# Low parts of 48 weight units: GpSimd's subtraction or an accumulating DMA, in a float32 conformer trunk

## The reference, cut to what matters

```
mod = silu(c) @ ada_w + ada_b                       # 6 vectors of 2048: shifts, scales, gates
h = rms_norm(x, norm1_g) * (1 + sc1) + sh1
u = h @ w_in + b_in ; a, gt = split(u)              # 2048 x 4096
u = a * sigmoid(gt)
u = causal depthwise conv, 31 taps + b_dw
u = silu(layer_norm(u)) ; y = u @ w_out + b_out     # 2048 x 2048
x = x + g1 * y
h = rms_norm(x, norm2_g) * (1 + sc2) + sh2
x = x + g2 * (square(relu(h @ w1)) @ w2)            # 2048 x 8192, 8192 x 2048
out = rms_norm(x, final_g)
```

## Time and profile before

| what | value |
|---|---|
| median of three runs | 2128.62 us |
| the profiled execution's own time | 2129.86 us |
| its span (first to last instruction) | 2128.1 us |
| mean granted TensorE clock | 0.968 |
| TensorE matmul busy | 2004.2 us (94%) x8640 |
| VectorE busy | 1097.9 us (52%) |
| ScalarE busy | 667.8 us (31%) |
| GpSimd busy | 451.1 us (21%) |
| DMA | 299.58 MB, mean 141 GB/s |

### The profile page before, as it was taken

The page is one execution under the profiler, slowest core; times in us unless marked ns, Lnnn a source line. Parts: engine busy times, 40 slices in busy tenths (PEclk is TensorE's granted clock), DMA queues, the critical chain, the costliest instruction groups (busy, mean ns, idle before and its releaser), DMA issues.

```text
span 2128.1 us, 22314 instructions
## 1 busy us (share of the span) xinstructions
PE 2004.2 (94%) x8640; PEld 1632.2 (77%) x8640; DVE 1097.9 (52%) x1133; ACT 667.8 (31%) x717; POOL 451.1 (21%) x197
## 2 busy tenths in 40 slices
PE   5889999888987889999999999999999999999996
PEld 2668888656766767888888888888888888888885
DVE  5959989978698984323323332332332332232243
ACT  4334545453232222232132123123213213312332
POOL 3647999923433230000000000000000000000001
PEclk8999999979998999999999999999999999999998
DMA  9962433315866572222222222222222222222212
GB/s 399 394 258 101 158 138 118 119 60 197 341 262 246 202 292 91 87 99 99 99 99 99 99 87 91 100 96 99 99 99 99 99 99 80 101 95 99 99 59 79
DMA packets 45933, 299.58 MB, mean 141 GB/s; under 512 B 4688, under 2 KB 4688, under 8 KB 10960
## 3 DMA queue, kind: packets, MB, share of 16 engines
q1 hardware_dynamic: 45904, 299.24, 37.5%
HBM read 295.03 MB, written 4.19 MB: 141 GB/s over the span
## 4 chain that ended last, share of the span: by engine, by line
PE 72%; DVE 13%; POOL 6%; issue 4%; DMA 3%; ACT 2%; SPq 0%; DVEq 0%; POOLq 0%; ACTq 0%
PE ps L313 23%; PE ps L314 23%; PE ps L315 23%; DVE adar L760 3%; POOL wlo L1055 3%; DMA adar<-ada 3%; DVE adar L772 2%; DVE raw L772 1%; POOL pacc L1094 1%; DVE hlo L766 1%; PE ps L386 1%; DVE ps L843 1%; POOL adar L1098 1%; DVE wlo L783 1%; ACT whi L472 1%
## 5 line engine op out<-in xcount | busy, mean ns | idle before, releaser
L313 PE MATMUL ps<-hhi,whi 128*128 128x512 f32 (+1 forms) x1792 | 708.6, 395 | 61.7 <-DVE hlo L766 29.8
L314 PE MATMUL ps<-hlo,whi 128*128 128x512 f32 (+1 forms) x1792 | 704.9, 393 | 0.0
L315 PE MATMUL ps<-hhi,wlo 128*128 128x512 f32 (+1 forms) x1792 | 704.4, 393 | 0.0
L472 ACT ACTIVATE whi<-raw 128x2048 fp32r<-128x2048 f32 x176 | 336.1, 1910 | 680.5 <-PE ps L315 680.5
L313 PEld LDWEIGHTS ps<-hhi,whi 128*128 128x128 f32 x1792 | 341.4, 191 | 141.0 <-issue 56.2
L313 PE MATMUL ps<-dhi,whi 128*128 128x512 f32 x1024 | 399.8, 390 | 11.7 <-DVE dlo L1020 11.7
L314 PE MATMUL ps<-dlo,whi 128*128 128x512 f32 x1024 | 399.6, 390 | 0.0
L315 PE MATMUL ps<-dhi,wlo 128*128 128x512 f32 x1024 | 399.3, 390 | 0.0
L315 PEld LDWEIGHTS ps<-hhi,wlo 128*128 128x128 f32 x1792 | 340.9, 190 | 72.2
L314 PEld LDWEIGHTS ps<-hlo,whi 128*128 128x128 f32 x1792 | 341.6, 191 | 70.7
L783 DVE TENSOR_TENSOR wlo<-raw,whi 128x2048 fp32r<-128x2048 f32 x127 | 291.0, 2292 | 95.6 <-ACT whi L472 95.6
(11 more groups left out here) (142 smaller groups left out, 951.3 us busy)
## 6 DMA issues: line engine op xcount, KB each, us to landing
raw<-w SPq DMA_DIRECT2D x176, 1024.0 KB, 4.8
adar<-ada SPq DMA_DIRECT2D x80, 1024.0 KB, 5.0
raw<-ada SPq DMA_DIRECT2D x16, 1024.0 KB, 8.5
xb<-xT SPq DMA_DIRECT2D x8, 1024.0 KB, 9.6
out<-xb SPq DMA_DIRECT2D x5, 512.0 KB, 4.3
out<-xb SPq DMA_DIRECT2D x6, 256.0 KB, 3.8
csb<-c SPq DMA_DIRECT2D x1, 1024.0 KB, 4.9
pr<-par SPq DMA_DIRECT2D x1, 368.0 KB, 14.3
```

The lines of the kernel that those rows point to most:

```text
L313: pe.matmul(out, whi[:, slot, t], xhi, start=first, stop=False, skip_group_check=True)
L314: pe.matmul(out, whi[:, slot, t], xlo, start=False, stop=False, skip_group_check=True)
L315: return pe.matmul(out, wlo[:, slot, t], xhi, start=False, stop=last, skip_group_check=True)
L472: act.activation(whi[:, q % WS, :], raw_slot(q), ACT.Copy).then_inc(whi_done, 1)
```

## The change

Units 10 to 57 (48 of the 49 that GpSimd subtracted) get their low part in another way: ScalarE writes the negated high part into `wlo` after it has written `whi`, and an accumulating DMA that GpSimd issues adds `raw` to it. Its semaphores are `lo_in[0..1]`. TensorE starts a unit at `whi_done` and waits for the low part only before the products that use it, which now stand last in every unit: in `outer_unit` all high-weight products with the high activations of a chunk, then those with its low part, for both chunks, and then the 16 low-weight products; in `inner_unit` 32 and then 16. The order of the products is changed in all 176 units, the way of the low part in 48. The waits of SyncE's loads follow the same semaphores. Loops are cut so that no loop holds units of both kinds, and one GpSimd loop is written out.

```diff
-LO_POOL = W2_0 + 2
+DMA_LO = range(A1 + 2, W2_0 + 2)
...
+        def wait_lo(eng, q, off=0):
+            if q in DMA_LO:
+                eng.wait_ge(lo_in[q % WS], 16 * ((q - DMA_LO.start) // WS + 1) + (16 // WS) * off)
+            else:
+                eng.wait_ge(wlo_done, (q + 1 if q < DMA_LO.start else q + 1 - len(DMA_LO)) + off)
...
             def load_unit(q, off=0):
-                sp.wait_ge(wlo_done, q - RAW + 1 + off)
+                wait_lo(sp, q - RAW, off)
...
+            def outer_unit(q, s, h0, j=0, i=None):
+                i, first = (0, s == 0 and j == 0) if i is None else (i, False)
+                pe.wait_ge(whi_done, 2 * i + (q + 2 * j + s + 1))
                 for kk in range(2):
-                    k = 4 * i + (2 * s + kk)
+                    k = 4 * i + (4 * j + 2 * s + kk)
+                    pe.wait_ge(hhi_done, k + (h0 + 1))
+                    for o in range(8):
+                        high(o, s, 8 * kk + o, ch(hhi, k), first and kk == 0)
                     pe.wait_ge(hlo_done, k + (h0 + 1))
                     for o in range(8):
-                        last = product(o, s, 8 * kk + o, ch(hhi, k), ch(hlo, k), first and kk == 0, False)
+                        high(o, s, 8 * kk + o, ch(hlo, k), False)
+                wait_lo(pe, q + 2 * j + s, 2 * i)
+                for kk in range(2):
+                    k = 4 * i + (4 * j + 2 * s + kk)
+                    for o in range(8):
+                        last = low(o, s, 8 * kk + o, ch(hhi, k), False)
                 last.then_inc(unit_done, 1)
...
+            def inner_unit(slot, bank, q, off=0):
+                pe.wait_ge(whi_done, off + (q + 1))
                 for k in range(KC):
-                    last = product(bank, slot, k, ch(hhi, k), ch(hlo, k), k == 0, k == KC - 1)
+                    high(bank, slot, k, ch(hhi, k), k == 0)
+                    high(bank, slot, k, ch(hlo, k), False)
+                wait_lo(pe, q, off)
+                for k in range(KC):
+                    last = low(bank, slot, k, ch(hhi, k), k == KC - 1)
                 last.then_inc(unit_done, 1)
...
                 act.activation(whi[:, q % WS, :], raw_slot(q), ACT.Copy).then_inc(whi_done, 1)
+                if q in DMA_LO:
+                    act.wait_ge(whi_done, q + 1 + off)
+                    act.activation(wlo[:, q % WS, :], f(whi[:, q % WS, :]), ACT.Copy, scale=-1.0
+                                   ).then_inc(neg_done, 1)
...
             def split_lo(q, off=0):
-                pool.wait_ge(whi_done, q + 1 + off)
-                pool.tensor_tensor(wlo[:, q % WS, :], raw[:, q % RAW, :], f(whi[:, q % WS, :]), ALU.subtract
-                                   ).then_inc(wlo_done, 1)
+                if q not in DMA_LO:
+                    pool.wait_ge(whi_done, q + 1)
+                    pool.tensor_tensor(wlo[:, q % WS, :], raw[:, q % RAW, :], f(whi[:, q % WS, :]), ALU.subtract
+                                       ).then_inc(wlo_done, 1)
+                    return
+                pool.wait_ge(neg_done, q - DMA_LO.start + 1 + off)
+                pool.dma_start(f(wlo[:, q % WS, :]), raw[:, q % RAW, :], accum_op=ALU.add
+                               ).then_inc(lo_in[q % WS], 16)
```

More of the change, by code:

```diff
@@ L134, in trunk_kernel @@
         wlo_done = sem("wlo_done")
+        neg_done = sem("neg_done")
+        lo_in = [sem(f"lo_in{i}") for i in range(WS)]
         unit_done = sem("unit_done")
@@ L266, in _ @@
             sp.wait_ge(ada_used, ADA0)
-            with loop(ET.SP, 0, 6) as i:
+            for s in range(2):
+                load_unit(A1 + 2 + 2 * s)
+                load_unit(A1 + 3 + 2 * s)
+                load_ada(2 * KC + s)
+            with loop(ET.SP, 0, 5) as i:
                 for s in range(2):
-                    load_unit(A1 + 2 + 2 * s, 4 * i)
-                    load_unit(A1 + 3 + 2 * s, 4 * i)
-                    load_ada(2 * KC + s, 2 * i)
+                    load_unit(A1 + 6 + 2 * s, 4 * i)
+                    load_unit(A1 + 7 + 2 * s, 4 * i)
+                    load_ada(2 * KC + 2 + s, 2 * i)
             a += ADA_A1
@@ L290, in _ @@
             assert a == ADA
-            load_unit(W2_0 + 2)
-            load_unit(W2_0 + 3)
-            with loop(ET.SP, 1, (NUNITS - W2_0) // RAW) as i:
+            for q in range(2, 6):
+                load_unit(W2_0 + q)
+            with loop(ET.SP, 0, (NUNITS - W2_0) // RAW - 2) as i:
                 for q in range(RAW):
-                    load_unit(W2_0 + q, 4 * i)
+                    load_unit(W2_0 + 6 + q, 4 * i)
+            load_unit(NUNITS - 2)
+            load_unit(NUNITS - 1)
             stores = [(fin_dve, n, min(2, FIN_POOL - n)) for n in range(0, FIN_POOL, 2)]
@@ L373, in _ @@
             outer_units(A0, 0)
-            with loop(ET.PE, 0, 6) as i:
+            for s in range(2):
+                pe.wait_ge(glu_done, 3 + s)
+                inner_unit(0, 2 * s, A1 + 2 * s)
+                inner_unit(1, 2 * s + 1, A1 + 2 * s + 1)
+            with loop(ET.PE, 0, 5) as i:
                 for s in range(2):
-                    pe.wait_ge(glu_done, 2 * i + (3 + s))
-                    inner_unit(0, 2 * s, 4 * i + (A1 + 2 * s + 1))
-                    inner_unit(1, 2 * s + 1, 4 * i + (A1 + 2 * s + 2))
+                    pe.wait_ge(glu_done, 2 * i + (5 + s))
+                    inner_unit(0, 2 * s, A1 + 4 + 2 * s, 4 * i)
+                    inner_unit(1, 2 * s + 1, A1 + 5 + 2 * s, 4 * i)
             for n, c in enumerate((KC - 2, KC - 1)):
@@ L426, in w2_unit, with w2_pairs @@
                             pe.wait_ge(dlo_done, wait_hidden + (k + 1))
-                        last = product(4 + 2 * (m % 2) + nn, m % 2, 8 * nn + k, ch(dhi, k), ch(dlo, k),
-                                       k == 0, k == BLK - 1)
+                        high(bank, m % 2, 8 * nn + k, ch(dhi, k), k == 0)
+                        high(bank, m % 2, 8 * nn + k, ch(dlo, k), False)
+                    if nn == 0:
+                        wait_lo(pe, q, off)
+                    for k in range(BLK):
+                        last = low(bank, m % 2, 8 * nn + k, ch(dhi, k), k == BLK - 1)
                 last.then_inc(unit_done, 1)
-            def w2_rest(b):
-                w2_unit(1, 16 * b + (W2_0 + 2))
+            def w2_pairs(b, q):
                 with loop(ET.PE, 1, 4) as i:
@@ L437, in w2_rest, with hidden_units @@
                         pe.wait_ge(x2_done, 16 * b + 4 * i + (2 * s - 1))
-                        w2_unit(s, 16 * b + 2 * i + (W2_0 + s + 1))
-            pe.wait_ge(wlo_done, W2_0 + 1)
+                        w2_unit(s, q + 2 + s, 16 * b + 2 * i - 2)
+            def hidden_units(b):
+                with loop(ET.PE, 0, 4) as i:
+                    for s in range(2):
+                        pe.wait_ge(relu_done, 8 * b + 2 * i + (BLK + s - 1))
+                        inner_unit(s, s, W2_0 + BLK + s, 16 * b + 2 * i)
+                pe.wait_ge(x2_done, 16 * b + 17)
+                w2_unit(0, W2_0 + 2 * BLK, 16 * b, 8 * b + BLK)
+            pe.wait_ge(whi_done, W2_0 + 1)
             pe.wait_ge(relu_done, 2)
@@ L445, in _ @@
                 for nn in range(2):
-                    last = product(4 + nn, 0, 8 * nn + k, ch(dhi, k), ch(dlo, k), n == 0, n == BLK - 1)
+                    high(4 + nn, 0, 8 * nn + k, ch(dhi, k), n == 0)
+                    high(4 + nn, 0, 8 * nn + k, ch(dlo, k), False)
+                    if n == 0 and nn == 0:
+                        wait_lo(pe, W2_0)
+                    last = low(4 + nn, 0, 8 * nn + k, ch(dhi, k), n == BLK - 1)
             last.then_inc(unit_done, 1)
             pe.wait_ge(relu_done, BLK)
[L449 to L457, removed]
+            w2_unit(1, W2_0 + 1)
+            w2_pairs(0, W2_0)
+            hidden_units(0)
+            with loop(ET.PE, 1, NBLK - 1) as b:
+                w2_unit(1, W2_0 + 2 * BLK + 1, 16 * b - 16)
+                w2_pairs(b, W2_0)
+                hidden_units(b)
+            w2_unit(1, W2_0 + 2 * BLK + 1, 16 * (NBLK - 2))
+            w2_pairs(NBLK - 1, W2_0)
             pe.wait_ge(ss2_done, KC)
@@ L1021, in _ @@
                                       ).then_inc(dlo_done, 1)
[L1022 removed]
+            dve.wait_ge(wlo_done, A1 + 2)
             with loop(ET.DVE, 0, NBLK - 1) as b:
@@ L1111, in _ @@
             a1_chunk(0, 1)
-            with loop(ET.Pool, 1, 4) as i:
+            for i in range(1, 4):
                 a1_chunk(i, 0)
@@ L1129, in _ @@
             c_sums(13)
-            for q in range(B0 + 2, LO_POOL):
+            for q in range(B0 + 2, DMA_LO.stop):
                 split_lo(q)
```

34 lines of the change are left out of this document (15 added, 19 removed).

## The result

The changed kernel takes 2158.6 us (median of 4, 2155.36 to 2160.9) against 2128.65 us (4 runs): ratio 1.0142, 95% interval 1.0126 to 1.0157, slower by 30 us. The forecast was 2143 us. The sign held, and most of the mechanism; one step failed: the stretch from B0's start to `x1` took 11.4 us more than before, where the sum had nothing. The profiled execution took 2155.36 us, the fastest of its four, 25.5 us above the profiled one of before.

What follows compares the result with a forecast made beforehand. Prediction: products bound A1 and the end; between 470 and 800 us `ada` loads and stalled VectorE reductions set the pace. Terms -1.9 + 0.4 + 18 - 1.4, less 2, gave +13 on 2129.86: 2143 us, range 2100 to 2190.

Steps and rivals of the forecast that it cites:

- The price: Each 1 MiB accumulating transfer was taken to occupy all DMA engines for 5.3 us, with 2.6 and 7.9 as ends.
- A0 and A1: Units 0 to 7 gain 1.9 us by product order; units 10 to 31 lose 0.4 us by a later convolution start.
- VectorE's stalls: GpSimd's subtraction stalls VectorE's two-input instructions; without it `ada` reductions stay at 2.28 us instead of up to 6.69.
- B0, up to unit 42: `x1` begins 5 us late, but lost stalls and a start without subtraction bring unit 42 forward: -1.5 us.
- Unit 36: In B0, TensorE starts at 518.0 instead of 522.85 us, but its low part comes at 529; about 3 us kept.
- B1: Seven more transfers make the last `ada` row 12 us later; a lost stall returns 4.2; C0's start +8 us.
- C0: Eight transfers beside the loads lengthen the stretch from 687 to 793 us to 116 instead of 106 us: +10.
- After W2: From the MLP's second matrix on, one stall goes and units 56 and 57 have early low parts: -1.4 us.
- -2 for shorter `hlo` waits: At the starts of B0 and C0, high products begin 0.7 us sooner and the slow clock ends sooner: -2 us.
- The cheap transfer: Rival: from B0 to C0 a transfer costs only 2.63 us and VectorE is free, giving 2102 us; chance 0.35.
- the low part comes late everywhere: Rival: TensorE waits before low products in all 48 units, about +60 us, 2190 us; chance 0.12 for dear or late.
- break-even price of 4.4 us: Transfer price at which the change neither gains nor loses, 2124 to 2136 us; chance 0.10 for a price near it.

Runs made afterwards that it cites:

- the plain copy: Changed kernel with a plain copy of `raw` into `wlo` instead of the accumulating transfer (output differs): 2114.48 us, 0.9935 of the kernel before.
- these transfers alone: New product order, with negation and accumulating transfer for units 42 to 57 only and GpSimd subtracting elsewhere: 2148.70 us, 1.0098 of the kernel before.
- without any maker: Changed kernel with its negations but neither transfer nor subtraction for the 48 low parts (output differs): 2084.39 us, 0.9788 of the kernel before.

## Why the prediction was right in kind and 15 us short

*The price.* Taken at 5.3 us, measured 5.20, and DMA's share from 530 to 790 us is 0.95, near full as the prediction required: right, and its three readings (2.6, 5.3, 7.9) were the right question, since the plain copy sits at 2.64. The Trainium skill's rule ("Collectives: The Full Stack", "The bandwidth ceiling: the fold count and why AG ≠ RS ≠ AR") that a reduce runs at half a copy's rate agrees with these two (1.97 times); its 31 GB/s, by which I had estimated 4.2 us, does not.

*A0 and A1* (-1.9 and +0.4). Unit 11's forward copy begins at 174.09 instead of 175.84 us: -1.75 of A0's -1.9. The convolution that began 11.24 us behind its `whi` begins 11.64 behind (338.67 against 327.03 us): +0.40 as worked out. B0 starts 0.8 us sooner, against -1.5, which is within what a mark can tell. For A1's end the number was luck: the prediction said that GpSimd's subtraction is one "that nobody waits for", and there the chain of before goes through it twice; the negation took its place.

*VectorE's stalls.* Reductions of 2282 to 2295 ns in all 51 from B0 to C0, with DMA at a share of up to 1.0 beside them: GpSimd was their whole cause. One reading beside it was wrong, without weight in the sum: of the 29.8 us in which TensorE waits for `hlo`, which the prediction named for 470 to 800 us, only 4.5 lie there.

*B0, up to unit 42* (-1.5). **This is the step that failed.** The prediction said that DMA near full would need "55 instead of 46 us, from 524 instead of 528", that `x1` begins 5 us late and unit 42 1.5 us early, and so let B1 start "from about 592 us as before". Measured: the chain starts at 518 and needs 67 us to `x1`; `x1` is 10.6 us late, unit 42 7.8 (609.2 us). First, the count was wrong, and the trace of before could have told it. I took 34 us for "ten rows and three units", by their number. But the window of the kernel before over that stretch says
```profile
528.00:574.00 46.00, 45.07 (x198) 36.91 (x198) 30.79 (x23) 8.08 (x5) 21.51 (x4) 1.00 0.82 315
```
0.82 x 46 = 37.7 us, the reloads of `xb` among them. And five transfers, not four, fall in the changed kernel's stretch from 518 on, as the one issued at 513.4 us is still under way: 37.7 + 5 x 5.2 = 63.7 us, where its window has 0.97 x 65 = 63. Second, even its own 5 us were not passed on: a lost stall and a start without a subtraction were set against them, for unit 42. But B1's rows follow from `x1`, which the `ada` rows alone set by then, and unit 42 could not use its early start, since TensorE waited 5.0 us for unit 41's low part (at 603.5 us).

*Unit 36.* Its low part was to keep TensorE waiting some 4 us; it waited 5.8.

*B1* (+12 - 4.2 = +8, from a start as before, 18 us behind `x1`) and *C0* (+10). From `x1` to C0 took 8.8 us more (9.8 with these transfers alone), from C0 to W2 8.7 more (8.3): both terms are right within 1.8 us. With `x1`'s 10.6 us at their head the two terms give C0 18.6 us late and W2 28.6; measured are 19.4 and 28.1. That a late B0 is not absorbed is the point of a full DMA: with GpSimd subtracting in B1 more than half of it was.

*After W2* (-1.4). From W2 to the end the profiled execution gained 2.6 us. Of the -2 for shorter `hlo` waits, 0.7 us shows at B0's start, where TensorE's wait fell from 5.65 to 4.93 us. It lies 25.5 us above the profiled execution of before, the medians 30; both profiled ones are single executions, and that of the changed kernel is its fastest.

*Rivals.* The cheap transfer's price stands in no run, but the plain copy has it, and gave 2114.5 us, not 2102. ScalarE's negations (15.5 us in the changed kernel) may be the difference; no run takes them out of the kernel with the plain copy. Its mechanism was real: the time without any maker is 2084. That the low part comes late everywhere did not happen; in A1 TensorE waited for one 0.3 us. The break-even price of 4.4 us is 3.5 by interpolation.

## What to carry to other kernels

Before a transfer is put where an engine worked, count DMA's busy time in that stretch from the window, all loads by their share and not the loads that come to mind, and look whether what follows has slack; if it has none, every microsecond is passed on, and none is absorbed. Ask not only whether the engine that is freed was the bound, but who else could do its work in less: here VectorE, whose stalls were the price of GpSimd's slower copy of the same instruction, did the work itself in 2.29 us and won 38.5 us, 2 of them by the new order. A copy added on an engine that looked idle, here ScalarE's 1.92 us, is not free either: ask whether it stands in a chain at a stage's end. An early stage with DMA at 0.89 and TensorE at its full pace shows that a busy resource costs next to nothing until somebody waits for it.

## What the runs showed of the hardware

- An accumulating transfer from SBUF to SBUF, 1 MiB with add, occupies all sixteen engines for 5.20 us; a plain one for 2.64. From issue to landing they took 11.0 and 5.1 us in the median beside the loads, and 0.87 and 0.55 us of GpSimd to issue.
- A load of 1 MiB (the `ada` rows issued from 505 us on) took 4.8 us from issue to landing in the median before and 10.0, up to 18.4, in the changed kernel with DMA's share at 0.86 to 1.00. The time of the loads' packets did not grow (37.5% of 2128.1 and 36.9% of 2153.3 us): the added time is spent before they are served.
- VectorE's reductions, with two SBUF inputs, were not slowed by DMA at a share of 1.0 (2.28 to 2.30 us, 51 of them); beside GpSimd's subtraction they took up to 6.69 us.
